# The chunk stream of a gated-DeltaNet layer: the inverse of each pair's second step shifted by half a period

## The reference

```
a_mat = jnp.where(strict, jnp.einsum("bhnid,bhnjd->bhnij", kb, k) * decay, 0.0)
sol = lax.linalg.triangular_solve(a_mat + eye, rhs, left_side=True, lower=True, unit_diagonal=True)
...
def step(s, inp):
    v_new = u_n - jnp.einsum("bhck,bhkv->bhcv", w_n, s)
    o = jnp.einsum("bhck,bhkv->bhcv", qd_n, s) + jnp.einsum("bhcj,bhjv->bhcv", qk_n, v_new)
    s = s * gt_n[..., None, None] + jnp.einsum("bhck,bhcv->bhkv", kt_n, v_new)
```

## Time and profile before

| | us |
|---|---|
| median of 3 runs | 3145.27 (3144.13 to 3149.03) |
| the profiled execution, its own time | 3154.63 |
| its span, first to last instruction | 3152.9 |
| TensorE busy in the span | 2707.3 (86%) |
| VectorE busy | 1758.6 (56%) |
| ScalarE busy | 1235.9 (39%) |
| GpSimd busy | 1183.8 (38%) |
| first matmul of the chunk stream | at 1822.1 |
| last matmul group of the chunk stream | at 2832.7 |

### The profile page before, as it was taken

How to read it: one execution, slowest core, us unless ns; L and a number is a source line. 1 busy time by engine, 2 the same in 40 slices (tenths; PEclk the granted TensorE clock), 3 DMA queues, 4 the chain that set the end, 5 groups by cost and what they waited for, 6 DMA issues and landing times. The chain is left out here.

```text
span 3152.9 us, 53264 instructions
## 1 busy us (share of the span) xinstructions
PE 2707.3 (86%) x18741; PEld 2594.3 (82%) x18741; DVE 1758.6 (56%) x2671; ACT 1235.9 (39%) x2107; POOL 1183.8 (38%) x1110
## 2 busy tenths in 40 slices
PE   4699999975997379999999789999999999985994
PEld 3699999975996269999999789998998999975993
DVE  3266666664300537777778646766666666654004
ACT  2255555554202224444444434454554544542001
POOL 3333333321230124444444334554444555433220
PEclk9899999987999779999999979999999999997996
DMA  3111111112413135555444451424233243214214
GB/s 111 48 54 50 51 53 48 50 36 75 149 63 139 51 73 154 148 152 153 147 144 142 117 153 44 106 55 106 76 76 106 45 115 105 47 28 159 77 47 162
DMA packets 249413, 292.60 MB, mean 93 GB/s; under 512 B 87419, under 2 KB 210892, under 8 KB 247580
## 3 DMA queue, kind: packets, MB, share of 16 engines
q1 hardware_dynamic: 244636, 273.35, 30.0%
q10 hardware_dynamic: 4608, 17.04, 1.7%
HBM read 194.30 MB, written 96.05 MB: 92 GB/s over the span
## 5 line engine op out<-in xcount | busy, mean ns | idle before, releaser
L1888 ACT ACTIVATE zz<-ps 104x416 fp32r<-104x416 f32 x560 | 286.9, 518 | 393.0 <-PE ps L1779 391.7
L543 PE MATMUL ps<-dn_yhi,dn_whi 128*128 128x416 f32 (+1 forms) x1152 | 395.2, 343 | 22.0 <-POOL dn_wlo L527 16.6
L1951 DVE TENSOR_TENSOR pp<-ps,level_mask 104x416 fp32r<-104x416 f32 x560 | 318.6, 586 | 124.4 <-PE ps L1779 123.6
L544 PE MATMUL ps<-dn_ylo,dn_whi 128*128 128x416 f32 (+1 forms) x1152 | 376.1, 326 | 0.0
L545 PE MATMUL ps<-dn_yhi,dn_wlo 128*128 128x416 f32 (+1 forms) x1152 | 375.9, 326 | 0.0
L543 PE MATMUL ps<-rg_yhi,rg_whi 128*128 128x416 f32 (+1 forms) x768 | 257.7, 336 | 82.4 <-DVE zs L829 41.7
L1781 PE MATMUL ps<-pp,zz 104*104 104x208 f32 x1440 | 267.2, 296 | 18.4 <-DVE pp L1951 16.0
L544 PE MATMUL ps<-rg_ylo,rg_whi 128*128 128x416 f32 (+1 forms) x768 | 256.8, 334 | 0.0
L545 PE MATMUL ps<-rg_yhi,rg_wlo 128*128 128x416 f32 (+1 forms) x768 | 255.8, 333 | 0.0
L1781 PE MATMUL ps<-zz,pp 104*104 104x208 f32 x1440 | 247.8, 282 | 0.0
L543 PEld LDWEIGHTS ps<-dn_yhi,dn_whi 128*128 128x128 f32 x1152 | 218.8, 190 | 28.4 <-POOL dn_wlo L527 17.0
(11 more groups left out here) (276 smaller groups left out, 7402.9 us busy)
## 6 DMA issues: line engine op xcount, KB each, us to landing
c_nq<-nq_scratch SPq DMA_DIRECT2D x160, 169.0 KB
dn_raw<-in_dn_w_in SPq DMA_DIRECT2D x48, 512.0 KB, 4.1
qd<-rows_scratch SPq DMA_DIRECT2D x160, 104.0 KB, 3.2
rg_raw<-in_rg_w_in SPq DMA_DIRECT2D x32, 512.0 KB, 3.9
nq_scratch<-p_nq SPq DMA_DIRECT2D x48, 338.0 KB
p_ex<-rows_scratch SPq DMA_DIRECT2D x32, 422.5 KB
nq_scratch<-p_rn SPq DMA_DIRECT2D x32, 338.0 KB
o_scratch<-a SPq DMA_DIRECT2D x16, 520.0 KB, 2.8
```

The source lines that it names most:

```text
L543: e.matmul(o, whi, mhi[:, t0:t0 + tn], start=(first and k == 0), stop=False)
L544: e.matmul(o, whi, mlo[:, t0:t0 + tn], start=False, stop=False)
L1888: e.activation(zz[:, b, :, :], ps[0:CH, 2 * b + 1, 0:m4], ACT.Copy).then_inc(zev.sem, 1)
L1951: e.tensor_tensor(D4(pp[:, b, l % 2, :, :]), D4(Y4), c["level_mask"][:, l, :, 0:CH].unsqueeze(2).to_broadcast([CH, 2, 2, CH]), ALU.mult).t ...
```

## The change

The inverse of the even step 2p keeps its slots. The inverse of the odd step 2p+1 starts five slots later (LAG = 5): parts 0 to 4 run in slots 5 to 9 of period p, parts 5 to 9 in slots 0 to 4 of period p+1. Within a slot the even step's part still comes first. State pieces, `pre`, `finish`, `final`, `tables`, all DMAs and the number and form of all compute instructions stay the same. As the parities no longer take turns, the four semaphores become eight, one of each kind for each parity, and `nth` counts within a parity.

```
+    LAG = SLOTS // 2
...
-        ym, yev, zm, zev = each("ym", YS), each("yev", YS), each("zm", ZS), each("zev", LEVELS)
+        ym, yev, zm, zev = ([S(f"{name}{b}", k * PAIRS * 2) for b in (0, 1)]
+                            for name, k in (("ym", YS), ("yev", YS), ("zm", ZS), ("zev", LEVELS)))
...
-            return g // 2 * 2 * k + 2 * i + g % 2 + 1
+            return g // 2 * k + i + 1
...
             for l in range(SLOTS):
-                for g in (2 * p, 2 * p + 1):
+                for g, part in ((2 * p, l), (2 * p + 1 if l >= LAG else 2 * p - 1, (l - LAG) % SLOTS)):
                     if lo <= g < hi:
-                        inverse(g, l)
+                        inverse(g, part)
...
-                        e.wait_ge(yev.sem, yev.at(n, nth(g, l - 1, YS)))
+                        e.wait_ge(yev[g % 2].sem, yev[g % 2].at(n, nth(g, l - 1, YS)))
                         if l >= 2:
-                            e.wait_ge(zev.sem, zev.at(n, nth(g, l - 2, LEVELS)))
+                            e.wait_ge(zev[g % 2].sem, zev[g % 2].at(n, nth(g, l - 2, LEVELS)))
...
-                        ins.then_inc(zm.sem, 1)
+                        ins.then_inc(zm[g % 2].sem, 1)
```

More of the change, by code:

```diff
@@ L1719, in pre @@
                     if g >= 4:
-                        e.wait_ge(zm.sem, zm.at(n, nth(g - 4, 0, ZS)))
+                        e.wait_ge(zm[g % 2].sem, zm[g % 2].at(n, nth(g - 4, 0, ZS)))
                     e.tensor_tensor(D4(nhr[:, g % 4, :, :]), v, eyes, ALU.add).then_inc(nt_done.sem, 1)
@@ L1728, in inverse @@
                     b = g % 2
-                    e.wait_ge(zev.sem, zev.at(n, nth(g, LEVELS - 1, LEVELS)))
+                    e.wait_ge(zev[g % 2].sem, zev[g % 2].at(n, nth(g, LEVELS - 1, LEVELS)))
                     if g >= 2:
@@ L1790, in inverse @@
                         if g >= 2:
-                            e.wait_ge(yev.sem, yev.at(n, nth(g - 2, YS - 1, YS)))
+                            e.wait_ge(yev[g % 2].sem, yev[g % 2].at(n, nth(g - 2, YS - 1, YS)))
                         for m in MS:
                             ins = widened(2 * b, m, nhr[:, q4, m, :], ident_r[:, :])
-                        ins.then_inc(ym.sem, 1)
+                        ins.then_inc(ym[g % 2].sem, 1)
                     elif l <= LEVELS:
                         old, p_ = nhr[:, q4] if l == 1 else zz[:, b], pp[:, b, (l - 1) % 2]
-                        e.wait_ge(yev.sem, yev.at(n, nth(g, l - 1, YS)))
+                        e.wait_ge(yev[g % 2].sem, yev[g % 2].at(n, nth(g, l - 1, YS)))
                         if l >= 2:
-                            e.wait_ge(zev.sem, zev.at(n, nth(g, l - 2, LEVELS)))
+                            e.wait_ge(zev[g % 2].sem, zev[g % 2].at(n, nth(g, l - 2, LEVELS)))
                         for m in MS:
                             ins = widened(2 * b, m, old[:, m, :], p_[:, m, :])
-                        ins.then_inc(ym.sem, 1)
+                        ins.then_inc(ym[g % 2].sem, 1)
                         if l == 1 and g >= 2:
@@ L1806, in inverse @@
                             ins = widened(2 * b + 1, m, p_[:, m, :], old[:, m, :])
-                        ins.then_inc(zm.sem, 1)
+                        ins.then_inc(zm[g % 2].sem, 1)
                     elif l == LEVELS + 1:
-                        e.wait_ge(yev.sem, yev.at(n, nth(g, LEVELS, YS)))
+                        e.wait_ge(yev[g % 2].sem, yev[g % 2].at(n, nth(g, LEVELS, YS)))
                         e.wait_ge(nt_done.sem, nt_done.at(n, 2 * g + 2))
@@ L1813, in inverse @@
                                            pp[:, b, LEVELS % 2, m, :].bitcast(F32), start=True, stop=True)
-                        ins.then_inc(ym.sem, 1)
+                        ins.then_inc(ym[g % 2].sem, 1)
                     else:
-                        e.wait_ge(yev.sem, yev.at(n, nth(g, LEVELS + 1, YS)))
+                        e.wait_ge(yev[g % 2].sem, yev[g % 2].at(n, nth(g, LEVELS + 1, YS)))
                         e.wait_ge(u_done.sem, u_done.at(n, g + 1))
@@ L1884, in inverse @@
                     b = g % 2
-                    e.wait_ge(zm.sem, zm.at(n, nth(g, l - 1, ZS)))
+                    e.wait_ge(zm[g % 2].sem, zm[g % 2].at(n, nth(g, l - 1, ZS)))
                     if l == 1 and g >= 2:
                         e.wait_ge(u_done.sem, u_done.at(n, g - 1))
-                    e.activation(zz[:, b, :, :], ps[0:CH, 2 * b + 1, 0:m4], ACT.Copy).then_inc(zev.sem, 1)
+                    e.activation(zz[:, b, :, :], ps[0:CH, 2 * b + 1, 0:m4], ACT.Copy).then_inc(zev[g % 2].sem, 1)
                 def state(g, piece):
@@ L1948, in inverse @@
                     if l <= LEVELS + 1:
-                        e.wait_ge(ym.sem, ym.at(n, nth(g, l, YS)))
+                        e.wait_ge(ym[g % 2].sem, ym[g % 2].at(n, nth(g, l, YS)))
                     if l < LEVELS:
@@ L1952, in inverse @@
                                         c["level_mask"][:, l, :, 0:CH].unsqueeze(2).to_broadcast([CH, 2, 2, CH]),
-                                        ALU.mult).then_inc(yev.sem, 1)
+                                        ALU.mult).then_inc(yev[g % 2].sem, 1)
                     elif l == LEVELS:
-                        e.tensor_tensor(pp[:, b, l % 2, :, :], Y4, eye, ALU.add).then_inc(yev.sem, 1)
+                        e.tensor_tensor(pp[:, b, l % 2, :, :], Y4, eye, ALU.add).then_inc(yev[g % 2].sem, 1)
                     elif l == LEVELS + 1:
                         e.scalar_tensor_tensor(pp[:, b, l % 2, :, :], Y4, 0.5, eye, ALU.mult, ALU.add) \
-                            .then_inc(yev.sem, 1)
+                            .then_inc(yev[g % 2].sem, 1)
                     else:
-                        e.wait_ge(zm.sem, zm.at(n, nth(g, ZS - 1, ZS)))
+                        e.wait_ge(zm[g % 2].sem, zm[g % 2].at(n, nth(g, ZS - 1, ZS)))
                         if g >= 2:
```

## The result

The changed kernel takes 3161.12 us (median of 5 runs, 3154.98 to 3163.0) against 3145.27 us before (5 runs, 3137.16 to 3151.39): a ratio of 1.0045, 95% interval 1.0024 to 1.0066. It is slower by 16 us; 3159 had been forecast. The profiled execution took 3161.8 us; this is the head of its page.

The account below looks back on a forecast made before the run. The prediction took TensorE to bound the kernel. Slots 4 to 5, slots 9 to 1, start and end summed as -15.0 + 27.5 - 1.5 + 3.1 = +14.1 us, giving 3159 us from the 3145.3 median; range 3142 to 3176.

Parts of the forecast that it names:

- Slots 4 to 6: Two groups move out, but TensorE stalls on the 1.15 us eviction latency; minus 0.385 us in 39 periods, minus 15.0 us.
- Slots 9 to 1: Six groups where there were four, O5 starting at 1.95 us; 3.44 us for 2.40, plus 1.04 in 24 regular periods.
- Periods with tables: Slot 9 to part 1 stays 4.18 us, set by VectorE's queue, so two extra groups are free: 0 in seven periods.
- the two turns of the loop: Counted among the seven tables periods, with a wait of 3.02 us for `pp`; cost 0.
- The first step of a head: Slot 9 to part 1 without a piece 0: 2.72 us after, 2.40 before, plus 0.32 us in eight periods.
- Slots 2 and 7, 0: The stall from `rr` ahead of the eviction neither goes nor grows; slot 7 still 2.86 us after piece 0; cost 0.
- Edges: First half period of the stream minus 1.5 us; its end, slot 9 of period 39 to first piece 2, plus 3.1 us.
- fewer drops: Rival: the granted clock drops less often in the stream; two drops gone turn +14 us into +4; chance 0.17.
- Another number of stretches at half: Sign in the clock column of the changed trace that the prediction would be wrong; no size given.
- More drops: Rival: new waits make the clock fall in five more periods, 25 us on top, 3184 us; chance 0.10.
- Even load: Rival: VectorE and ScalarE get work evenly, TensorE's waits for them vanish in 39 periods; minus 54 us, 3091; chance 0.05.
- Mostly covered: Rival: the new stalls are real but overlapped, for example by weight loads, each costing half; 3145 us; chance 0.13.

Follow-up runs that it names:

- LAG = 5, second set: The changed kernel run again unaltered beside more runs of the kernel before: 3164.01 us against 3146.82, ratio 1.0057.
- LAG = 5, odd first: The changed kernel with the odd step's part before the even one's in slots 5 and 9 on all engines: 3148.87 us, ratio 0.9994.
- before_rr: The kernel before, with VectorE doing the `rr` of pieces 0 one slot later, in slots 1 and 6: 3124.26 us, ratio 0.9948.
- half_best: The changed kernel with odd part first in slots 5 and 9, `rr` one slot later, `sq` in slots 4 and 9, tables in slot 2: 3111.42 us.
- best: The kernel before (lockstep) with `rr` one slot later, `sq` in slots 4 and 9, and tables in slot 2: 3106.75 us, ratio 0.9872.

## Why the prediction was right, and where its sum was not

**Slots 4 to 6, minus 0.385 us: right.** E4 to E5 is 1.89 us behind a `sq` and 1.56 without, E5 1.15 to 1.17 us after E4's Z group. In period 20 slots 5 to 6 take 1.91 us in place of 2.29.

**Slots 9 to 1, plus 1.04 us: right in kind, short by 0.11.** O5 started at 2.05, not 1.95: `zz` was ready at 2324.05, which the walk had at about that time, but the Y group began 0.14 us later where 0.03 to 0.05 had been taken for the signal. In 24 periods that is 2.6 us. The first step of a head has 2.84 us where 2.72 was forecast.

**Periods with tables, 0: right where VectorE sets the pace.** In period 18 TensorE is timed by VectorE as before:

```profile
2271.73 0.52 PE L1783 MATMUL ps<-uu,pp 104*104 104x208 f32 x3
...
2273.77 0.51 PE L1783 MATMUL ps<-pp,zz 104*104 104x208 f32 x3 [0.32 <-ACT zz L1890]
...
2275.93 0.53 PE L1783 MATMUL ps<-pp,nhr 104*104 104x208 f32 x3 [0.30 <-DVE pp L1953]
```

It takes 4.20 us, 4.18 in the earlier trace rows, with two more groups inside. The wait ahead of part 1 has fallen from 1.56 us to 0.30. But the 4.18 us rest on one instruction of the tables that took 1.04 us (see the last section). In other executions it took 0.18: then the stretch is 3.32 us in the kernel with LAG = 0 and 3.54 in the second profile of the changed one (period 18), TensorE is no longer timed by VectorE, and the change costs 0.22 us there, not 0. The profiled execution of the changed kernel has the short one in period 8.

The prediction put the two turns of the loop under the same kind. They are another one: in the changed kernel TensorE does not wait for VectorE there. The profile shows two gaps that it puts down to nothing (period 23, from part 0 to piece 0):

```profile
2398.24 0.53 PE L1783 MATMUL ps<-ident_r,nhr 104*104 104x208 f32 x3 [2.10 <-issue]
...
2401.84 2.03 PE L1836 MATMUL ps<-st,c_qk 128*104 128x256 f32 x4 [2.26 <-issue]
```

**Slots 2 and 7, 0: right.** Slot 7 of period 20 still comes 2.86 us after piece 0.

**Edges.** The first half period gave 0.9 us for 1.5 forecast. From slot 9 of period 39 to the first piece 2 it is 2827.88 - 2819.16 = 8.72 us, the walk's number, but the rest of the tail is 1.2 us longer too. Nearly all of that is not the order but the clock: from 2836 us on this execution has a clock of 0.57, while the kernel before ran the same last groups at 1.00.

**The sum was right by two errors that cancel, so its closeness is in part luck.** Here are the periods, each from the start of the Y group of part 1 in the period before to that in the period named, worked out from the timelines:

| periods | before | after | difference | forecast |
|---|---|---|---|---|
| 20 (regular) | 24.45 | 25.27 | +0.82 | +0.655 |
| 21 (first step) | 23.54 | 23.65 | +0.11 | -0.065 |
| 22 (regular) | 22.98 | 23.82 | +0.84 | +0.655 |
| 18 (tables) | 26.06 | 25.85 | -0.21 | -0.385 |
| 19 (regular) | 23.72 | 24.49 | +0.77 | +0.655 |

Each is 0.12 to 0.19 us above the forecast: 0.11 is the late O5 (0.02 in the period with tables), and the rest are hundredths in other slots that the walk put at nothing. A head costs 2.4 us more where 1.5 was forecast, and over the stream, with the edges, the order costs about 20 us, not 14. The other error is the clock. I put a change of the drops down as a rival and took none for the forecast. In the profiled pair the drops of the stream fell from four to two (44 us at the half clock to 17). At the half clock TensorE's work takes up to twice as long, so 27 us less of it are worth up to 13 us, which is most of why the spans differ by 7 us only; the short instruction of the tables in two periods of the changed kernel gives another 1 to 2 us. The rival "fewer drops" came true in part, and the mechanism of the forecast as well. Another number of stretches at half was also one of the prediction's own signs of being wrong, and it came.

**The clock, run by run.** Of the 25 runs of the kernel before in one session, those at a mean clock of 0.928 took 3150.3 to 3153.8 us and those at 0.935 took 3135.8 to 3137.6; a line through each of the three sessions has a slope of 1.7 to 2.4 us for 0.001. With 2 us for 0.001 the ratios can be set at equal clock:

| kernel | ratio gives us | mean clock, this and before | at equal clock | walk |
|---|---|---|---|---|
| LAG = 5, second set | +17.9 | 0.9320, 0.9308 | +20 | +14 |
| LAG = 3 | +5.0 | 0.9358, 0.9306 | +15 | +15 |
| LAG = 1 | +9.8 | 0.9344, 0.9306 | +17 | +18 |
| LAG = 5, odd first | -1.9 | 0.9324, 0.9306 | +2 | -7 + 6 |
| LAG = 0 | +0.3 | 0.9322, 0.9315 | +2 | 0 |

(In the fourth row -7 is the forecast 14 - 21, and 6 what the walk of LAG = 5 was short of.) At equal clock the three lags cost about the same, as the trace of periods 15 to 19 has it too, and the differences between them are those of the clock. The 2 us for 0.001 are the slope within one kernel; that it holds from one kernel to another is taken, not shown. That the clock is higher because a long wait of TensorE ahead of part 1 is broken up is only argued: near period 3 the profiles have a drop in three kernels, all of them in lockstep with the tables ahead of slot 0 (before, LAG = 0, before_rr), and in none of the others; near period 33 only the kernel before has one, and LAG = 0 has none after the same stretch of 4.19 us. Moving the tables did not settle it. At the turns of the loop the prediction's reading, a drop after the wait for the tables, is not what the rows show. In period 23 of the kernel before the clock falls behind a gap put down to "issue", and the wait for `pp` comes only then:

```profile
2394.97 0.55 PE L1781 MATMUL ps<-ident_r,nhr 104*104 104x208 f32 x3 [2.03 <-issue]
...
2395.41 0.81 PE L1781 MATMUL ps<-ident_r,nhr 104*104 104x208 f32 x3
...
2400.61 0.85 PE L1781 MATMUL ps<-pp,nhr 104*104 104x208 f32 x3 [2.51 <-DVE pp L1951]
```

The second group takes 0.81 us where it takes 0.50 at the full clock.

**The rivals.** "More drops" did not happen. "Even load" is refuted by half_best against best. "Mostly covered" is refuted by the rows above: the Z latency shows in full in slots 4 to 5, and a little more than that in slots 9 to 0, where two groups stand between a Z group's start and the next part of its step.

## What to carry to other kernels

When two chains hide each other's latency, write down for each hand-over the latency and the work that stands behind it; here it was 1.155 us of cover for 1.15 us, and a regrouping that puts a short part beside a full one, with nothing else between, left 0.4 us bare, even though it was meant to make each engine's load more even. Count the cover lost as well as the cover won when a piece is moved, and try the order of neighbours within a slot first, since it adds no work and here brought back the whole measurable loss. Look for what an in-order queue does ahead of an eviction: moving four `rr`, one `sq` and a head's tables behind the evictions brought 1.3% in lockstep and, with the odd part first, 1.1% at half a period, where the lag by itself brought nothing.

## What the runs showed of the hardware

The half clock holds on while TensorE is busy. In the earlier trace rows TensorE is busy for 10.00 of 10 us at 0.50, and the changed kernel has 9.04 of 10 us at 0.52 after the loop's turn. In both the DMA share is high, 0.98 and 1.03, which the prediction held against its rival of fewer drops. But a high share does not bring the half clock by itself: here is a stretch of the kernel before, as busy and with as much DMA, at the full clock.

```profile
2030.00:2040.00 10.00, 10.00 (x97) 9.82 (x95) 6.27 (x16) 4.76 (x12) 4.43 (x7) 1.00 1.00 280
```

The Trainium skill ("TensorE: Matmul & The Clock Gate", Part 1) has activity release the slow clock; these rows have activity without release, and the cause stays open.

A 104x40 VectorE instruction of the tables (L1938, L1940 in the changed kernel) takes 0.18 us or 1.04 to 1.07 us, in the same kernel too, from one period or execution to the next. In the kernel before, period 18, it began while GpSimd's product on `c_vo` ran and ended with it:

```profile
2273.71 1.11 POOL L1764 TENSOR_TENSOR c_vo<-c_vo,c_zs 128x416 f32<-128x416 f32 x1 [2.52 <-DVE c_vo L2008]
...
2273.82 1.04 DVE L1938 TENSOR_SCALAR head_eg<-eg 104x40 f32 x1
```

In period 8 of the changed kernel the same pair runs the other way, with VectorE at 0.18 and GpSimd at 1.22 us:

```profile
2021.51 1.22 POOL L1766 TENSOR_TENSOR c_vo<-c_vo,c_zs 128x416 f32<-128x416 f32 x1 [3.57 <-DVE c_vo L2010]
...
2021.62 0.18 DVE L1940 TENSOR_SCALAR head_eg<-eg 104x40 f32 x1
```

A product on `c_vo` takes 1.07 us in the median, so in either case one of the two holds the other up. Where it is VectorE, part 1 of that period is 0.87 us later in the lockstep kernels (4.19 against 3.32 us from slot 9), in up to seven periods of an execution. The Trainium skill ("GPSIMD Engine Reference", section 1, Specifications) says that GpSimd shares its interfaces to SBUF with VectorE and contends with VectorE instructions in a 2-port mode or with two inputs from SBUF. The rows agree in that the two do not run independently here; in which mode this instruction ran no row shows.
